# Six weight chunks held outside the ring, router logits taken from the residual rows, and the last norm done tile by tile

## The chip, the cores and the metric

The kernel runs on one core of one Trainium2 chip. The metric is device time in microseconds (us) of the whole kernel, lower is better. TensorE (PE) multiplies, VectorE (DVE) and ScalarE (ACT) do the elementwise work, SyncE (SP) issues most transfers, and 16 DMA engines move data between the device memory and the on-chip arena.

## What is computed

The program is two blocks in a row on 256 tokens of width 1024, all in f32: a transformer block of two layers, then a block of two layers whose second half is a mixture of experts. The change touches only the mixture of experts and the norm at the very end:

```
def ec_moe(h, router, wg, wu, wd):
    aff = softmax(h @ router)                      # 256 tokens x 16 experts
    gates, idx = top_k(swapaxes(aff, 1, 2), 32)    # each expert picks 32 tokens
    xs = h[idx]
    hid = silu(xs @ wg) * (xs @ wu)                # per expert, 1024 x 1024 each
    ys = hid @ wd * gates
    return zeros.at[idx].add(ys)
...
hx = rmsnorm_2(x, norm_g[i, 1]) * (1.0 + sc2x) + sh2x
x = x + g2x * ec_moe(hx, ...)
...
return rmsnorm_2(x, final_g)
```

Layer 0 runs this for two streams (x and ctx, four tiles of 128 tokens), the last layer for x alone (two tiles).

## The kernel before, in words

Weights come as one stream of chunks of 1 MB (128 partitions x 2048 f32) in the order of their use. `stream_weights` lets SP load them into a ring of six slots (`RING = 6`): SP waits on `chunks_used` until the chunk six places earlier has been read by PE, then issues the next transfer. PE waits for a chunk in `wait_chunk`. No other rule decides when a weight is loaded.

`experts(layer, ...)` is one stage of 4 + 192 chunks, each engine with its own program in written order, tied by the counting semaphores in `self.moe`:

- PE: `project(t)` multiplies by the output matrix of the mixer (4 chunks) for tile t; `turn_row(t)` transposes the normed tile `xn`; `logits(t)` multiplies the features `hT` by the router (8 products, which the trace shows as 16 PE instructions). Then come the turn of the softmax, `gate_rows`, and the first `gather` of tokens. Then 16 experts follow with 12 chunks each: chunks 0 to 3 (gate), 4 to 7 (up), 8 to 11 (down). `sum_expert(e - 1, ...)`, which scatters the expert before into the output banks, stands ahead of chunk 8.
- DVE adds the projected tile to the residual row (L1931, L1932), makes rstd and the normed tile, and does the softmax and the choice of tokens. ACT squares the row (L1877), takes the root, and writes the features out of PSUM with the scale and shift of the modulation, in 8 instructions of 128 columns for a tile (L1882). It issues the stage's small loads at its start (L1713, L1714).
- At the end `final_norm` starts with a `meet` of the engines (a wait on every semaphore so far), loads the gain `final_g` (L1469), squares both tiles, takes the mean, root and reciprocal of both, scales both (L368), and multiplies both by the gain (L1478). `store` has another `meet` on SP and then two transfers (L3189).

The clock of PE has two levels, 2.4 GHz (shown as a granted clock of 1.00) and 1.2 GHz (0.50).

## Time and profile before

| what | value |
|---|---|
| median of 3 runs | 3271.4 us (3271.13 to 3273.81) |
| the profiled execution's own time | 3272.74 us |
| its span, first to last instruction | 3270.7 us |
| PE busy, share of the span | 2856.5 us, 87% |
| DVE and ACT busy | 1155.4 us (35%), 999.8 us (31%) |
| mean granted clock of PE | 0.939 |
| moved by DMA | 708.64 MB, mean 217 GB/s |

The averages hide stages with different limits: the first two layers are full of PE work, and the two stages of experts stream 192 MB of weights each. The stage of layer 0 spans about 1448 to 2034 us, the last stage about 2712 us to the end. What an edit in one of them is worth has to be read there.

### The profile page before, as it was taken

What the parts mean: (1) busy time and instruction counts of PE and PEld (TensorE: products, weight loads), DVE (VectorE), ACT (ScalarE), POOL (GpSimd) and SP (SyncE); (2) the same over time, 40 slices, a digit from 0 to 9 for tenths busy, and PEclk for the clock granted to TensorE, in tenths of its full rate; (3) what the DMA queues carried; (4) which work ended last, traced back from release to release, by engine and by line L of the source; (5) the groups of instructions that cost most, each with busy time, mean ns of one, the idle gap of its engine ahead of it and who ended that gap; (6) DMA issues with size and microseconds to landing.
All of it is one profiled execution on the core that took longest, in us unless ns stands there. A gap on an engine that the chain in (4) does not pass through costs nothing.

```text
span 3270.7 us, 63075 instructions
## 1 busy us (share of the span) xinstructions
PE 2856.5 (87%) x27786; PEld 1880.1 (57%) x27786; DVE 1155.4 (35%) x1567; ACT 999.8 (31%) x1549; POOL 172.7 (5%) x229
## 2 busy tenths in 40 slices
PE   8999899999998899998998888998888887677765
PEld 6777677778676777755333223346777764332322
DVE  4445555455355565422000002334444433000001
ACT  4435544444345455323000001114444422000000
POOL 0001000000002000000000000002222210000000
PEclk9999999999999999998999999999999998777776
DMA  6463234565642354402999999611000014999997
GB/s 252 167 262 129 104 145 171 198 244 182 263 154 98 121 212 161 176 27 97 422 421 421 421 421 375 257 60 60 15 10 16 4 35 164 421 421 420 421 421 295
DMA packets 100989, 708.64 MB, mean 217 GB/s; under 512 B 11604, under 2 KB 12372, under 8 KB 17280
## 3 DMA queue, kind: packets, MB, share of 16 engines
q1 hardware_dynamic: 94320, 682.34, 52.8%
q10 hardware_dynamic: 5760, 19.91, 1.6%
q8 instruction: 219, 3.59, 0.4%
q0 software_dynamic: 656, 2.52, 0.2%
q14 instruction: 34, 0.28, 0.0%
HBM read 703.65 MB, written 1.07 MB: 215 GB/s over the span
## 4 chain that ended last, share of the span: by engine, by line
PE 63%; DMA 21%; DVE 6%; ACT 5%; issue 3%; POOL 1%; SPq 0%; DVEq 0%; ACTq 0%; POOLq 0%
DMA weight_ring<-in_stream 21%; PE banks L641 8%; PE banks L643 7%; PE banks L642 7%; PE banks L1859 7%; PE banks L2135 3%; PE banks L1740 3%; PE banks L957 3%; PE banks L959 2%; PE banks L958 2%; PE banks L2181 2%; PE banks L2554 1%; PE banks L2541 1%; PE banks L1086 1%; PE banks L2545 1%
## 5 line engine op out<-in xcount | busy, mean ns | idle before, releaser
L1859 PE MATMUL banks<-weight_ring,scratch 128*32 128x256 f32 (+1 forms) x4608 | 638.0, 535 | 185.8 <-DMA weight_ring<-in_stream 181.9
L1859 PEld LDWEIGHTS banks<-weight_ring,scratch 128*32 128x32 f32 (+1 forms) x4608 | 201.4, 134 | 603.1 <-DMA weight_ring<-in_stream 295.6
L638 DVE TENSOR_TENSOR split_high<-weight_ring,split_high 128x1024 fp32r<-128x1024 f32 x198 | 243.5, 1231 | 282.0 <-ACT split_high L633 280.6
L633 ACT CAST split_high<-weight_ring 128x1024 fp32r<-128x1024 f32 x198 | 207.9, 1052 | 312.6 <-PE banks L643 262.9
L1974 DVE TENSOR_TENSOR scratch<-scratch,banks 128x512 f32<-128x512 f32 (+1 forms) x32 | 17.7, 555 | 604.1 <-PE banks L1859 604.1
L1280 DVE TENSOR_TENSOR split_high<-weight_ring,split_high 128x1024 fp32r<-128x1024 f32 x128 | 160.0, 1256 | 199.1 <-ACT split_high L1175 198.7
L2883 ACT COPY scratch<-banks 128x512 f32<-128x512 f32 (+2 forms) x208 | 153.3, 767 | 230.0 <-PE banks L2545 132.2
L641 PE MATMUL banks<-split_high,features_low 128*128 128x512 f32 x528 | 210.8, 399 | 3.5 <-DVE features_low L560 3.5
L643 PE MATMUL banks<-split_high,features_high 128*128 128x512 f32 x528 | 207.3, 393 | 0.0
L642 PE MATMUL banks<-split_high,features_high 128*128 128x512 f32 x528 | 206.9, 392 | 0.0
L957 PE MATMUL banks<-split_high,features_low 128*128 128x512 f32 x416 | 170.6, 410 | 19.5 <-DVE split_high L1280 16.3
L1175 ACT CAST split_high<-weight_ring 128x1024 fp32r<-128x1024 f32 x128 | 133.2, 1047 | 135.6 <-PE banks L959 134.1
L1906 ACT ACTIVATE scratch<-banks 128x512 f32<-128x512 f32 (+1 forms) x32 | 15.7, 490 | 517.1 <-PE banks L1859 517.1
L958 PE MATMUL banks<-split_high,features_high 128*128 128x512 f32 x416 | 165.4, 398 | 0.0
L959 PE MATMUL banks<-split_high,features_high 128*128 128x512 f32 x416 | 165.3, 397 | 0.0
L1908 ACT COPY scratch<-banks 128x512 f32<-128x512 f32 (+1 forms) x32 | 15.3, 479 | 353.7 <-PE banks L1835 353.7
L638 DVE TENSOR_TENSOR scratch<-weight_ring,scratch 128x1024 fp32r<-128x1024 f32 x66 | 80.8, 1225 | 107.7 <-ACT scratch L633 107.4
L641 PEld LDWEIGHTS banks<-split_high,features_low 128*128 128x128 f32 x528 | 99.9, 189 | 26.4 <-issue 4.0
L643 PEld LDWEIGHTS banks<-split_high,features_high 128*128 128x128 f32 x528 | 99.9, 189 | 21.3
L642 PEld LDWEIGHTS banks<-split_high,features_high 128*128 128x128 f32 x528 | 100.0, 189 | 20.9
L641 PE MATMUL banks<-split_high,scratch 128*128 128x512 f32 x264 | 106.7, 404 | 2.8 <-DVE scratch L764 2.8
L957 PEld LDWEIGHTS banks<-split_high,features_low 128*128 128x128 f32 x416 | 80.0, 192 | 44.2 <-DVE split_high L1280 21.7
(381 smaller groups left out, 4687.5 us busy)
## 6 DMA issues: line engine op xcount, KB each, us to landing
weight_ring<-in_stream SPq DMA_DIRECT2D x648, 1024.0 KB, 11.3
scratch<-in_pair_rows ACTq DMA_DIRECT2D x8, 448.0 KB, 3.7
scratch<-in_lora ACTq DMA_DIRECT2D x2, 1536.0 KB, 17.1
front<-in_gain_rows ACTq DMA_DIRECT2D x5, 512.0 KB, 3.7
bias<-bias_rows POOLq DMA_DIRECT2D x1, 2304.0 KB, 13.7
scratch<-in_routing ACTq DMA_DIRECT2D x2, 1040.5 KB, 5.4
resid<-in_x SPq DMA_DIRECT2D x2, 512.0 KB, 3.9
resid<-in_ctx ACTq DMA_DIRECT2D x2, 512.0 KB, 5.6
```

Source lines behind the costliest of these rows:

```text
L633: act.copy(split[i % 4][0], source(i)).then_inc(*self.rounded.up())
L638: dve.tensor_tensor(lo, source(i), hi.bitcast(F32), ALU.subtract).then_inc(*self.rest.up())
L641: pe.matmul(out, lhs_lo, hi, start=start, stop=False)
L642: pe.matmul(out, lhs_hi, lo, start=False, stop=False)
L643: return pe.matmul(out, lhs_hi, hi, start=False, stop=stop)
L957: pe.matmul(out, lhs_lo, hi, start=start, stop=False)
L958: pe.matmul(out, lhs_hi, lo, start=False, stop=False)
L959: return pe.matmul(out, lhs_hi, hi, start=False, stop=stop)
L1175: act.copy(split[i % 3][0], source(i)).then_inc(*self.rounded.up())
L1280: dve.tensor_tensor(lo, source(i), hi.bitcast(F32), ALU.subtract).then_inc(*self.rest.up())
L1859: last = pe.matmul(self.psum[q * M:(q + 1) * M, (GATE, UP, DOWN)[part], 0:W], left, w[:, j * D + q * W:j * D + (q + 1) * W], start=(k == 0 ...
L2883: act.copy(dst, src).then_inc(*done.up())
```

## The change

Four things change, all but the last two in `experts`.

1. Chunks 6 to 11 of expert 0 of the last stage are taken out of the stream. They are an input of their own, `kept`, and ACT loads them at the begin of the stage into six free pieces of the arena. PE reads them there; the stream has six chunks less, so chunk 0 of expert 1 follows chunk 5 of expert 0 in the ring.
2. The logits are made from the residual row before its norm: `turn_row` transposes `row(t)` and waits for `rowed` where it waited for `normed`; ACT copies the transposed tile in one instruction; DVE scales the router once (`scaled`) and afterwards multiplies the logits by rstd and adds an offset, the product of shift and router, for which PE has 8 more products for each stream (`offsets`).
3. `sum_expert(e - 1, ...)` moves from ahead of chunk 8 to ahead of chunk 4.
4. The last norm: its gain is loaded with the stage's small loads, the squares of a tile start as its row is ready, and gain and rstd are applied by one instruction for a tile. SP waits for each tile alone.

```diff
-        gate = [A[:, 30780 + D * s:30780 + D * (s + 1)] for s in range(S)]
+        gate = [A[:, 30780 + D * s:30780 + D * (s + 1)] for s in range(2)] if layer == 0 else [A[:, 28864:29888]]
+        kept = [A[:, o:o + CHUNK] for o in ((6144, 14336, 2048, 10240, 29888, 31936) if layer else ())]
...
+            else:
+                act.dma_start(gain, io["final_g"].to_broadcast([P, D])).then_inc(*self.params_loaded.dma())
+                for i, w in enumerate(kept):
+                    act.dma_start(w, io["kept"][i]).then_inc(*self.kept_loaded[i // 2].dma())
...
             def turn_row(t):
-                wait(pe, "normed", t + 1)
+                wait(pe, "rowed", t + 1)
...
+            def offsets(s):
+                if s == 0:
+                    wait(pe, "scaled", 1)
+                for k in range(KT):
+                    pe.matmul(self.psum[:, 0 if S == 2 else 4, (n_t + s) * NE:(n_t + s + 1) * NE], self.modcol[:, 3, s, k:k + 1].to_broadcast([P, P]),
+                              router[:, k, :], start=(k == 0), stop=(k == KT - 1))
...
+            for s in range(S):
+                offsets(s)
             turn_row(n_t - 1)
             logits(n_t - 2)
             logits(n_t - 1)
...
                     if c == 4 and e:
                         wait(pe, "weighted", e)
+                        wait(pe, "ys", e)
+                        for t in range(1 if S == 2 else TT):
+                            sum_expert(e - 1, t, SUM)
...
-                        if e:
-                            wait(pe, "ys", e)
-                            for t in range(1 if S == 2 else TT):
-                                sum_expert(e - 1, t, SUM)
                         wait(pe, "hid_saved", e + 1)
...
-                    n = e0 + 12 * e + c
-                    self.wait_chunk(pe, n)
-                    w = self.slot(n)
+                    at = 12 * e + c
+                    n = e0 + at - (0 if at < RING else len(kept))
+                    own = not RING <= at < RING + len(kept)
+                    if own:
+                        self.wait_chunk(pe, n)
+                        w = self.slot(n)
+                    else:
+                        pe.wait_ge(self.kept_loaded[(at - RING) // 2].sem, 32)
+                        w = kept[at - RING]
...
-                for k in range(KT):
-                    last = act.activation(hT[:, k, t * P:(t + 1) * P], self.psum[:, 2 * t + k // 4, (k % 4) * P:(k % 4 + 1) * P],
-                                          ACT.Identity, bias=self.modcol[:, 3, s, k:k + 1], scale=self.scol[:, 1, s, k:k + 1])
-                last.then_inc(*up("featured"))
+                act.copy(hT[:, :, t * P:(t + 1) * P].rearrange("p (a k) c -> p a k c", a=2),
+                         self.bank(2 * t, 2).rearrange("p a (k c) -> p a k c", k=4)).then_inc(*up("featured"))
...
+            dve.wait_ge(self.params_loaded.sem, loaded)
+            for s in range(S):
+                last = dve.tensor_tensor(scaled[:, s], router, bc(self.scol[:, 1, s, :], NE), ALU.mult)
+            last.then_inc(*up("scaled"))
             for t in range(n_t):
...
             wait(dve, "logits", 1)
-            then(dve.tensor_reduce(by_tile[0], logits, AX.X, ALU.max))
-            dve.tensor_tensor(aff, logits, bc(by_tile[0], NE), ALU.subtract).then_inc(*up("less_max"))
+            dve.tensor_copy(offset, self.psum[:, 0 if S == 2 else 4, n_t * NE:(n_t + S) * NE].rearrange("p (s e) -> p s e", s=S)).then_inc(*self.ve.up())
+            then(dve.tensor_tensor(aff, by_stream, bc(rstd.rearrange("p (s t) -> p t s", s=S), NE), ALU.mult))
+            then(dve.tensor_tensor(aff, aff, offset.unsqueeze(1).to_broadcast([P, TT, S, NE]), ALU.add))
+            then(dve.tensor_reduce(by_tile[0], aff, AX.X, ALU.max))
+            dve.tensor_tensor(aff, aff, bc(by_tile[0], NE), ALU.subtract).then_inc(*up("less_max"))
...
+                def scale(t):
+                    dve.wait_ge(self.row_rooted.sem, norm0[self.row_rooted] + t + 1)
+                    then(dve.reciprocal(rstd[:, t:t + 1], roots[:, t:t + 1]))
+                    dve.scalar_tensor_tensor(out=out[:, t, :], in0=row(t), scalar=rstd[:, t:t + 1], in1=gain, op0=ALU.mult, op1=ALU.mult)\
+                        .then_inc(*self.row_normed.up())
+
+                finish(0)
+                finish(1)
+                mean(0)
+                scale(0)
+                mean(1)
+                scale(1)
...
         @self.block.sync
         def _(sp):
-            self.meet(sp)
             for t in range(TT):
+                self.outputs(sp, t)
                 sp.dma_start(io["out"][t * P:(t + 1) * P], out[:, t, :]).then_inc(*self.stored.dma())
```

Three places show how the instructions move. The first is PE in layer 0, from the transposes of tile 2 on to the softmax's turn. L1750 (L1743 in the changed kernel) is `turn_row`, L1759 (L1752) `logits`, L1761 `offsets`. Before:

```order
L1750 MATMUL banks<-ident,scratch_0 128x128 x8
L1759 MATMUL banks<-scratch_0 128x16 x8
L1750 MATMUL banks<-ident,scratch_0 128x128 x8
L1759 MATMUL banks<-scratch_0 128x16 x16
L1801 MATMUL banks<-ident,small 32x128 x2
```

and in the changed kernel:

```order
L1743 MATMUL banks<-ident,resid 128x128 x8
L1752 MATMUL banks<-scratch_0 128x16 x8
L1761 MATMUL banks<-scratch_0,small 128x16 x16
L1743 MATMUL banks<-ident,resid 128x128 x8
L1752 MATMUL banks<-scratch_0 128x16 x16
L1803 MATMUL banks<-ident,small 32x128 x2
```

The 16 products of the offsets stand ahead of the transposes of the last tile, where PE had nothing queued. The last stage has the same order with half as many (8).

The second place is PE in expert 0 of the last stage, from chunk 5 to chunk 0 of expert 1, with its waits. L1859 (L1866) is the expert product; a wait on `slot_loaded` is one for the ring. Before:

```order
L1859 MATMUL banks<-weight_ring,scratch_0 32x256 [waits slot_loaded5]
L1859 MATMUL banks<-weight_ring,scratch_0 32x256 x7
L1859 MATMUL banks<-weight_ring,scratch_0 32x256 [waits slot_loaded0]
L1859 MATMUL banks<-weight_ring,scratch_0 32x256 x7
L1859 MATMUL banks<-weight_ring,scratch_0 32x256 [waits slot_loaded1]
L1859 MATMUL banks<-weight_ring,scratch_0 32x256 x7
L1772 MATMUL banks<-scratch_0 128x128 [waits moe_selected,moe_silu]
L1772 MATMUL banks<-scratch_0 128x128 x3
L1835 MATMUL banks<-ident,scratch_0 128x128 [waits moe_hid]
L1835 MATMUL banks<-ident,scratch_0 128x128
L1859 MATMUL banks<-weight_ring,scratch_0 32x256 [waits slot_loaded2,moe_hid_saved]
```

and in the changed kernel:

```order
L1866 MATMUL banks<-weight_ring,scratch_0 32x256 [waits slot_loaded5]
L1866 MATMUL banks<-weight_ring,scratch_0 32x256 x7
L1866 MATMUL banks<-scratch_0 32x256 [waits kept_loaded0]
L1866 MATMUL banks<-scratch_0 32x256 x7
L1866 MATMUL banks<-scratch_0 32x256 [waits kept_loaded0]
L1866 MATMUL banks<-scratch_0 32x256 x7
L1772 MATMUL banks<-scratch_0 128x128 [waits moe_selected,moe_silu]
L1772 MATMUL banks<-scratch_0 128x128 x3
L1840 MATMUL banks<-ident,scratch_0 128x128 [waits moe_hid]
L1840 MATMUL banks<-ident,scratch_0 128x128
L1866 MATMUL banks<-scratch_0 32x256 [waits kept_loaded1,moe_hid_saved]
```

PE's work is the same, but the six chunks 6 to 11 no longer wait for the ring; their waits are on `kept_loaded0` to `kept_loaded2`.

The third place is DVE from the last sums to its last instruction. Before (L1990 and L1991 add an output tile to the residual row, L368 scales by rstd, L1478 by the gain):

```order
L1990 TENSOR_TENSOR scratch_0<-banks,scratch_0 128x1024
L1991 TENSOR_TENSOR resid<-resid,scratch_0 128x1024
L1990 TENSOR_TENSOR scratch_0<-banks,scratch_0 128x1024
L1991 TENSOR_TENSOR resid<-resid,scratch_0 128x1024
L350 UNCONDITIONAL_BRANCH
L354 TENSOR_SCALAR small<-small 128x2
L362 UNCONDITIONAL_BRANCH
L365 RECIPROCAL small<-small 128x2
L368 TENSOR_SCALAR scratch_0<-resid,small 128x1024 x2
L1478 TENSOR_TENSOR scratch_0<-scratch_0 128x1024 x2
```

and in the changed kernel:

```order
L2014 TENSOR_TENSOR scratch_0<-banks,scratch_0 128x1024
L2016 TENSOR_TENSOR resid<-resid,scratch_0 128x1024
L2020 TENSOR_SCALAR small<-small 128x1
L2024 RECIPROCAL small<-small 128x1
L2025 SCALAR_TENSOR_TENSOR scratch_0<-resid,small,scratch_0 128x1024
L2020 TENSOR_SCALAR small<-small 128x1
L2024 RECIPROCAL small<-small 128x1
L2025 SCALAR_TENSOR_TENSOR scratch_0<-resid,small,scratch_0 128x1024
```

Four long instructions after the last sum become two, and each tile has its own mean and reciprocal.

## Rows read from the trace of the kernel before

In rows of the timeline the first two numbers are the start and the length in us, then engine, line, operation, output<-input and count; in brackets is the idle time before and what ended it. In rows of windows they are the stretch, its length, the busy time (and count) of PE, PEld, DVE, ACT and POOL, the granted clock of PE, the busy share of the DMA engines, and GB/s.

**Rows 1.** The page: GB/s moved, in 40 equal slices of the span

```profile
GB/s 252 167 262 129 104 145 171 198 244 182 263 154 98 121 212 161 176 27 97 422 421 421 421 421 375 257 60 60 15 10 16 4 35 164 421 421 420 421 421 295
```

**Rows 2.** Windows: one in each stage of experts, and two near the end

```profile
1900.00:2000.00 100.00, 84.06 (x374) 24.72 (x370) 6.86 (x12) 4.14 (x7) 0.00 (x0) 1.00 1.01 421
...
2900.00:3000.00 100.00, 70.92 (x740) 30.40 (x730) 5.68 (x13) 5.22 (x15) 0.00 (x0) 0.75 1.01 421
...
3246.00:3248.00 2.00, 1.89 (x33) 0.89 (x32) 0.95 (x3) 0.00 (x0) 0.00 (x0) 1.00 0.03 8
```

**Rows 3.** Timeline of expert 0 and the first ring rounds of the last stage

```profile
2775.05 5.39 PE L1859 MATMUL banks<-weight_ring,scratch 128*32 128x256 f32 x96 [0.90 <-ACT scratch L1898]
2776.33 53.57 SPq L328 DMA_DIRECT2D weight_ring<-in_stream  x25
...
2785.07 1.93 PE L1859 MATMUL banks<-weight_ring,scratch 128*32 128x256 f32 x16 [2.81 <-DMA weight_ring<-in_stream]
...
2799.98 1.07 PE L1859 MATMUL banks<-weight_ring,scratch 128*32 128x256 f32 x16 [1.31 <-DMA weight_ring<-in_stream]
...
2814.91 1.07 PE L1859 MATMUL banks<-weight_ring,scratch 128*32 128x256 f32 x16 [0.58 <-DMA weight_ring<-in_stream]
```

**Rows 4.** Timeline of layer 0, from the logits of tile 1 to the softmax

```profile
1507.55 1.86 PE L1759 MATMUL banks<-scratch 128*128 128x16 f32 x16
...
1508.13 1.23 DVE L1932 TENSOR_TENSOR resid<-resid,scratch 128x1024 f32<-128x1024 f32 x1
...
1513.14 1.97 PE L1750 MATMUL banks<-ident,scratch 128*128 128x128 f32 x8 [3.74 <-DVE scratch L1937]
...
1514.91 6.84 PE L1759 MATMUL banks<-scratch 128*128 128x16 f32 x32
...
1521.79 0.23 DVE L1942 TENSOR_REDUCE small<-banks 128x4 f32<-128x64 f32 x1 [8.70 <-PE banks L1759]
```

**Rows 5.** Timeline of the last stage, from the transposes of tile 0 to the softmax

```profile
2743.57 1.04 PE L1750 MATMUL banks<-ident,scratch 128*128 128x128 f32 x8
...
2745.03 1.22 DVE L1932 TENSOR_TENSOR resid<-resid,scratch 128x1024 f32<-128x1024 f32 x1
2747.39 1.09 ACT L1877 ACTIVATE scratch<-resid 128x1024 f32<-128x1024 f32 x1
...
2750.04 1.97 PE L1750 MATMUL banks<-ident,scratch 128*128 128x128 f32 x8 [5.44 <-DVE scratch L1937]
...
2758.69 0.19 DVE L1942 TENSOR_REDUCE small<-banks 128x2 f32<-128x32 f32 x1 [8.70 <-PE banks L1759]
```

**Rows 6.** Windows of 5 us over the same places of both stages

```profile
1510.00:1515.00 5.00, 1.85 (x10) 1.86 (x10) 1.07 (x3) 1.89 (x5) 0.00 (x0) 0.53 0.23 98
1515.00:1520.00 5.00, 5.00 (x26) 5.00 (x25) 0.00 (x0) 4.18 (x9) 0.00 (x0) 0.50 0.00 0
...
2745.00:2750.00 5.00, 0.00 (x0) 0.00 (x0) 2.30 (x4) 3.78 (x11) 0.00 (x0) 0.93 0.50 197
```

**Rows 7.** Timeline of the last expert and what follows it

```profile
3239.87 2.09 PE L1785 MATMUL banks<-scratch 32*128 32x256 f32 x16
...
3253.31 1.23 DVE L1991 TENSOR_TENSOR resid<-resid,scratch 128x1024 f32<-128x1024 f32 x1
...
3263.09 2.36 DVE L1478 TENSOR_TENSOR scratch<-scratch 128x1024 f32<-128x1024 f32 x2
3266.39 0.83 SPq L3189 DMA_DIRECT2D out_x<-scratch  x2
```

**Rows 8.** One line's instructions: durations in ns, least, median, most

```profile
L554 DVE SCALAR_TENSOR_TENSOR front<-resid,small,front x12: 1283/1285/1286, 11.0 to 1183.3; 128x1024 f32<-128x1024 f32 x12
```

**Rows 9.** Timeline at the begin of the last stage: loads by ACT

```profile
2730.30 0.46 ACTq L1714 DMA_DIRECT2D scratch<-in_routing  x1
```

**Rows 10.** DMA issues: count, KB each, median us to landing

```profile
scratch<-in_lora ACTq DMA_DIRECT2D x2, 1536.0 KB, 17.1
scratch<-in_routing ACTq DMA_DIRECT2D x2, 1040.5 KB, 5.4
```

More of the change, by code:

```diff
@@ L243, in __init__ @@
         self.early |= {"ctx_turned": self.moe["row_turned"], "gate_saved": self.moe["gate_saved"], "row_finished": self.moe["rowed"]}
+        self.kept_loaded = [signal(f"kept_loaded{i}") for i in range(3)]
         self.rowed = signal("row_ready")
@@ L1459 @@
     MOD = 34064
-    def final_norm(self, name, dst):
-        nc, ve = self.nc, self.ve
-        xn, gain = self.tiles(0, TT, D), self.arena[:, 2048:3072]
-        @self.block.scalar
-        def _(act):
-            self.meet(act)
-            act.dma_start(gain, self.io[name].to_broadcast([P, D])).then_inc(*self.params_loaded.dma())
-        loaded = self.params_loaded.count
-        self.norm_rows([0, 1], xn)
-        @self.block.vector
-        def _(dve):
-            dve.wait_ge(ve.sem, ve.count)
-            dve.wait_ge(self.params_loaded.sem, loaded)
-            for t in range(TT):
-                nc.vector.tensor_tensor(dst(t), xn[:, t, :], gain, ALU.mult).then_inc(*ve.up())
     def ada_chunk(self, pe, chunk, k, cT, bank):
@@ L1699, in experts @@
         tile_of = [(s, t) for s in range(S) for t in range(TT)]
+        gain, out = A[:, 17408:18432], self.tiles(0, TT, D)
         base = {n: s.count for n, s in self.moe.items()}
+        norm0 = {s: s.count for s in (self.rowed, self.row_squared, self.row_meant, self.row_rooted, self.row_normed)}
         before = self.so_far()
@@ L1870, in _ @@
                 last.then_inc(*up("summed"))
-        self.chunk = e0 + MOE_CHUNKS
+        self.chunk = e0 + MOE_CHUNKS - len(kept)
         @self.block.scalar
@@ L1911, in _ @@
             act.activation(self.small[:, 16:17], self.ident[:, 0:1], ACT.Sqrt).then_inc(*self.se.up())
+            if S == 1:
+                for t in range(TT):
+                    act.wait_ge(self.rowed.sem, norm0[self.rowed] + t + 1)
+                    act.activation(out[:, t, :], row(t), ACT.Square, accum_out=sums[:, t:t + 1]).then_inc(*self.row_squared.up())
+                for t in range(TT):
+                    act.wait_ge(self.row_meant.sem, norm0[self.row_meant] + t + 1)
+                    act.activation(roots[:, t:t + 1], sums[:, t:t + 1], ACT.Sqrt).then_inc(*self.row_rooted.up())
         @self.block.vector
@@ L1972, in _ @@
                 wait(dve, "silu", e + 1)
-                dve.wait_ge(self.chunks_used.sem, e0 + 12 * e + 8)
+                if kept and e == 0:
+                    wait(dve, "kept_up", 1)
+                else:
+                    dve.wait_ge(self.chunks_used.sem, e0 + 12 * e + 8 - len(kept))
                 dve.tensor_tensor(hid[:, e % 2, 0:W], silu[:, e % 2, 0:W], self.psum[:, UP, 0:W], ALU.mult).then_inc(*up("hid"))
@@ L1978, in _, with finish, mean @@
                                          op0=ALU.is_equal, op1=ALU.mult).then_inc(*up("weighted"))
-                dve.wait_ge(self.chunks_used.sem, e0 + 12 * e + 12)
+                if kept and e == 0:
+                    wait(dve, "kept_down", 1)
+                else:
+                    dve.wait_ge(self.chunks_used.sem, e0 + 12 * e + 12 - len(kept))
                 dve.tensor_copy(ys[:, e, :], self.psum[:, DOWN, 0:W]).then_inc(*up("ys"))
-            for i in range(S):
+            if S == 1:
+                def finish(t):
+                    wait(dve, "summed", TT)
+                    then(dve.tensor_tensor(xn[:, t, :].rearrange("p (q d) -> p q d", q=Q), self.psum[:, SUM:SUM + Q, t * W:(t + 1) * W],
+                                           gate[0].rearrange("p (q d) -> p q d", q=Q), ALU.mult))
+                    dve.tensor_tensor(row(t), row(t), xn[:, t, :], ALU.add).then_inc(*self.rowed.up())
+                def mean(t):
+                    dve.wait_ge(self.row_squared.sem, norm0[self.row_squared] + t + 1)
+                    dve.tensor_scalar(sums[:, t:t + 1], sums[:, t:t + 1], 1.0 / D, EPS, ALU.mult, ALU.add).then_inc(*self.row_meant.up())
+                def scale(t):
[9 more added lines that the diff above has]
+                scale(1)
```

45 lines of the change are left out of this document (26 added, 19 removed).

## The prediction, made before the changed kernel ran

> **What bounds the kernel now.** I read the page's slices first: both stages of experts run at 421 to 422 GB/s, the rest far below [rows 1]. The windows say what PE does meanwhile: in layer 0 it is busy 84 of 100 us at full clock, in the last stage 71 of 100 us at a mean clock of 0.75, and the DMA engines are at 1.01 in both [rows 2]. So the stream bounds these stages, with PE slack, and what counts is when the stream starts to run and how many chunks it has. Then the timeline at both ends. In the last stage PE starts expert 0 at 2775.05 with six chunks in the ring, SP issues the next at 2776.33, and from then on PE waits for DMA: the chunk at 2799.98 and the one six later at 2814.91 are 14.93 us apart, 2.49 us a chunk [rows 3]. Ahead of that stands the routing, a chain of small work in which the stream is idle: no byte moves in 1515 to 1520 us [rows 6]. Behind it stands a tail in which nothing is loaded.
>
> **1. Six chunks outside the ring.** PE reads chunks 0 to 5 and 6 to 11 of expert 0 without the ring; the ring restarts at the same point, but has 180 chunks instead of 186. If it never runs dry, the last chunk lands 6 x 2.49 = 14.9 us earlier. One condition: the seventh new chunk needs the slot of chunk 0 of expert 1, so PE must be through expert 0 before the six slots are full. The chunk of 2799.98 is the eighth after the restart, so the sixth lands at 2795.0, 19.9 us after PE's start, and SP must issue the next some 2 us before. PE needs 5.4 us for chunks 0 to 5, then six more at 1.07 us (full clock, as at 2799.98) or 1.93 us (half, as at 2785.07) [rows 3], the gather, two turns and spread, some 3 to 5 us, and 1 to 2 us for chunk 0 of expert 1: 16 us at full clock, 23 us at half. PE is at full clock there before and has no wait now, so I take 16 and no stall. Bounds: 14.9 us to 14.9 - 5.3 us.
>
> The six transfers are issued by ACT from about 2731 us on, behind the stage's small loads. With four ring chunks they are 10 MB, 25 us at 421 GB/s, so all is there by 2757 us, and the first kept chunk is read after 2776. The idle stream hides them. The DMA page of the Trainium skill ("DMA: Bandwidth & Descriptors", Bandwidth) has loads from HBM held to about 358 GB/s for a core; by that a chunk were 2.93 us and the six worth 17.6 us, and the time 2.7 us lower. This trace's 421 GB/s contradicts it, and the trace decides.
>
> **2. Logits from the residual row, last stage: 4.4 us gained.** Now tile 1's row is ready at 2745.03 + 1.22 = 2746.25, and PE stands until 2750.04 for square, root and normed tile; transposes and 32 logit instructions then run at half clock, and DVE starts the softmax at 2758.69 [rows 5]. After: PE ends tile 0's transposes at 2744.6 [rows 5], then the offsets: 16 instructions. At full clock one takes 1.86 / 16 = 0.116 us, at half 6.84 / 32 = 0.214 us [rows 4]. So offsets to 2746.5, transposes of tile 1 to 2747.55 (1.04 us as tile 0's), logits of tile 0 from there. ACT squares the row in 1.09 us [rows 5] and copies the features by 2749.1, in time. The clock is the open point. In layer 0 PE ran the last projection, transposes and 1.86 us of logits [rows 4], and the clock fell in the window 1510 to 1515 (0.53); the last stage's fell near the end of 2745 to 2750 (0.93) [rows 6]. And PE stood at 0.50 while busy 5.00 of 5.00 us with logits [rows 6]: this work didn't raise it. So I let the clock fall amid the logits, at about 2748.5: 8 instructions at 0.116, 24 at 0.214, end 2753.6, against 2758.69. That is 5.1 us. DVE has three more small instructions (0.19 to 0.23 us each [rows 4, 5] and the step between them): 0.7 us back. Sum 4.4 us; bounds 1.3 (all at half clock) and 6.7 us (all at full).
>
> **3. The same in layer 0: 2.4 us lost.** Here the offsets are 32 instructions, and tile 3's row is ready at 1508.13 + 1.23 = 1509.36, just as PE ends the logits of tile 1 at 1509.41 [rows 4]. The offsets go first. Before, the transposes started at 1513.14 [rows 4]. With the clock falling near 1511, 14 offsets at full and 18 at half clock take 5.5 us, to 1514.9: 1.8 us later than before, and the rest runs at half clock as it did. With 0.7 us for DVE that is 2.4 us lost. Bounds: 3.8 us lost (all at half) and 3.2 us gained (all at full: offsets 3.7, transposes 1.04, logits 3.7 us, end 1517.9 against 1521.79, less 0.7).
>
> The new wait: DVE waits at the head of the stage for all small loads before it makes the scaled router, and tile 0's row is queued behind it, then PE's transposes. In layer 0 the loads have 13 us of projection ahead. In the last stage routing is issued at 2730.30 [rows 9] and lands in 5.4 us [rows 10]; the gain behind it is 0.5 MB more, 1.2 us, and ring chunks share the engines from about 2733, so 2738.5. Router and tile 0's row take 2.7 us more, to 2741.2; PE wants it at 2743.57 [rows 5]. Hidden, with 2.4 us to spare. ACT spends some 3 us more on issuing, and its square for tile 0 has until 2744. Costed at nothing.
>
> **4. sum_expert earlier.** It leaves the end of each expert: 2.09 us in the last one [rows 7]. Inside the stages the stream hides both places. In the last expert of either stage chunk 8 starts earlier, until the hidden tile's copy, and in the last stage until chunk 11's landing: almost nothing moves after 3246 (8 GB/s [rows 2]), so about there. I take 0.8 us for both stages; bounds 0 and 3.
>
> **5. The tail: 7.4 us.** The last sum's row ends at 3253.31 + 1.23 = 3254.54, the span at 3270.7: 16.2 us, with the gain's load, the squares, two passes over both tiles, the meet, and two stores [rows 7]. After: square of tile 1 to 3255.75 (tile 0's ran beside the sums), root and reciprocal 0.4, one fused pass of 1.28 [rows 8] to 3257.5, mean, root and reciprocal of tile 1 0.6, pass of 1.28 to 3259.4. From the issue of the second store to the end before: 3270.7 - 3266.81 = 3.9 us [rows 7], so 3263.3. Gain 7.4 us; bounds 6 and 8.
>
> **Sum.** 14.9 + 4.4 - 2.4 + 0.8 + 7.4 = 25.1 us. The profiled execution took 3272.7 us, so 3247.6; it is 1.3 us above the median of 3271.4, so 3246.3 us.
>
> **The rivals.**
>
> A. The clock stays up through the routing, as PE now has no gap. Layer 0 then gains 3.2 instead of losing 2.4, the last stage 6.7 instead of 4.4: 7.9 us more, 3238.4 us. For it: no idle time is left between projection and logits. Against: [rows 6], as above. The Trainium skill's page "TensorE: Matmul & The Clock Gate" (Part 1) has the clock given back by sustained activity and taken by idleness, which speaks for this case; the busy 1515 to 1520 us at 0.50 speak against it. Chance 0.13.
>
> B. The ring runs dry behind expert 0, because PE needs 23 us at half clock: 5.3 us lost, 3251.6 us. Against: full clock there in the trace. Chance 0.12.
>
> C. The small loads of the last stage land late and DVE's new wait exceeds its cover. Loads queued by ACT together can take 17.1 us (lora, [rows 10]); then row 0 comes at 2750.6, 7 us after 2743.6: 3253.3 us. "DMA: Bandwidth & Descriptors" of the Trainium skill (Queues, rings and completion order) lets every DMA engine alternate between queues, which makes the ring a competitor here; no row shows the shares. Chance 0.10.
>
> D. The stage isn't as free as it looks: PE becomes the bound once the stream is ahead, and the six chunks bring nothing. Then 3261.2 us. Against: PE's 29 idle us of 100 [rows 2]. Chance 0.05.
>
> E. Slower: the kept transfers crawl. At lora's 1.57 MB in 17.1 us, 92 GB/s, 6.3 MB take 68 us, the last pair lands at 2799 and PE, which would start expert 0 at 2770.6, wants it 12 us later: 16 to 17 us late, of which the ring forgives 3, so 3246.3 + 14 = 3260. It decides below 79 GB/s (80 us, 28 late, all 25 us gone); at 70 GB/s it is 38 late, 3246.3 + 35 = 3281 us. Against: lora was one of four loads issued together beside the ring. Chance 0.03.
>
> **Numbers.** The forecast has 0.55; the 0.02 left I give to no change that can be told. Its own range is 3242 to 3251. For 8 in 10 I add most of A and C: 3239 to 3253. A measurement of this kernel can tell about 0.2%, 6.5 us: only E lies on the slow side, and D is 10 us off and still faster. Faster 0.95, within 0.2% 0.02, slower 0.03.
>
> **What would show it.** Right: in the last stage SP's issues run without a pause after expert 0, chunk cadence 2.49 us, and from PE's start of expert 0 to the last chunk 14.9 us less; no wait on the kept chunks; offsets between transposes in both stages, with 0.116 and then 0.214 us each; the softmax of layer 0 about 2 us later than before, counted from the last projection, and that of the last stage 5 us earlier; about 8.8 us from the last sum to the end. Wrong: a wait of DVE for loads that reaches past 2743.6, a hole in the stream some 20 us after expert 0 starts, full clock through the logits, or a wait for a kept chunk.

## The result and the profile after

The changed kernel took 3242.5 us in the median of 4 runs (3237.7 to 3250.2), the kernel before 3271.6 us (3271.1 to 3273.8) beside it: a ratio of 0.9907, 95% interval 0.9894 to 0.9921. The forecast was 3246.3, its own range 3242 to 3251. The profiled execution took 3243.30 us, 29.44 us less than the 3272.74 of the one before.

To see where they come from I cut each profile at eight events of the timelines: start and end of layer 0's projection (the first transposes behind it), the Exp of its softmax, PE's first product of its expert 0, and in the last stage the transposes of tile 0, the Exp, expert 0, the last DVE copy of an expert, the last residual add, and the span's end. In us:

| stretch | before | after | gained |
|---|---|---|---|
| up to layer 0's projection (untouched) | 1448.10 | 1447.21 | 0.89 |
| that projection (untouched) | 58.57 | 58.58 | 0.0 |
| layer 0: transposes to Exp | 15.64 | 16.49 | -0.85 |
| layer 0: Exp to expert 0 | 18.63 | 20.28 | -1.65 |
| layer 0's experts to the last stage's transposes | 1202.63 | 1201.22 | 1.4 |
| last stage: transposes to Exp | 15.57 | 8.89 | 6.7 |
| last stage: Exp to expert 0 | 15.91 | 14.54 | 1.4 |
| expert 0 to the last copy: the stream | 472.91 | 459.44 | 13.5 |
| last copy to last add | 5.35 | 5.86 | -0.5 |
| last add to the end | 17.4 | 8.9 | 8.5 |

**The six chunks.** Below is the timeline of PE and of SP's queue from expert 0 of the last stage on, after; it answers to [rows 3].

```profile
2767.21 5.39 PE L1866 MATMUL banks<-weight_ring,scratch 128*32 128x256 f32 x96 [0.90 <-ACT scratch L1908]
2772.42 1.91 PE L1866 MATMUL banks<-scratch 128*32 128x256 f32 x32
...
2780.77 3.64 PE L1866 MATMUL banks<-weight_ring,scratch 128*32 128x256 f32 x64
...
2787.35 1.07 PE L1866 MATMUL banks<-weight_ring,scratch 128*32 128x256 f32 x16 [0.87 <-DMA weight_ring<-in_stream]
2789.81 1.07 PE L1866 MATMUL banks<-weight_ring,scratch 128*32 128x256 f32 x16 [1.40 <-DMA weight_ring<-in_stream]
...
2768.49 45.85 SPq L330 DMA_DIRECT2D weight_ring<-in_stream  x22
```

PE reads chunks 0 to 5, then two kept ones at 2772.42 with no wait; the other four, at 2776.10 and 2779.02, wait for no load either. It is at chunk 0 of expert 1 at 2780.77, 13.6 us after its start, so that slot is free about 14.5 us after it, where 16 was forecast and some 18 were allowed. The waits for DMA begin at 2787.35 and stand 2.5 us apart, as before, with no hole. The kept transfers are issued from 2731.49 on; their landings, and that of the gain, stand in the answer on DMA issues between 2720 and 2800 (KB each, median us to landing):

```profile
scratch<-in_kept ACTq DMA_DIRECT2D x6, 1024.0 KB, 22.3
...
scratch<-in_final_g ACTq DMA_DIRECT2D x1, 512.0 KB, 7.2
```

Before, the ring was full by about 2748 and nothing moved until PE began expert 0. The window of before, with the DMA share and GB/s in its last two columns:

```profile
2750.00:2775.00 25.00, 19.00 (x80) 16.37 (x80) 7.37 (x26) 8.64 (x19) 0.00 (x0) 0.60 0.00 1
```

The windows after, two over layer 0's routing and four over the last stage's, show that idle stream in use (up to about 2761.5; the forecast had 2757 and left out the small loads), and in front of the last two columns PE's granted clock, on which the next parts rest:

```profile
1510.00:1515.00 5.00, 5.00 (x32) 5.00 (x31) 0.92 (x2) 0.57 (x2) 0.00 (x0) 0.63 0.04 16
1515.00:1520.00 5.00, 5.00 (x25) 5.00 (x25) 0.00 (x0) 1.80 (x2) 0.00 (x0) 0.50 0.00 0
...
2745.00:2750.00 5.00, 4.99 (x46) 4.89 (x45) 2.51 (x5) 4.13 (x6) 0.00 (x0) 1.00 1.02 429
2750.00:2755.00 5.00, 3.06 (x14) 2.35 (x14) 2.11 (x10) 0.51 (x2) 0.00 (x0) 0.54 1.01 419
2755.00:2760.00 5.00, 2.46 (x4) 0.52 (x2) 4.62 (x15) 1.01 (x1) 0.00 (x0) 0.78 1.02 423
2760.00:2765.00 5.00, 4.18 (x24) 4.08 (x25) 1.09 (x5) 1.24 (x4) 0.00 (x0) 0.66 0.33 136
```

**The last stage's routing.** The timeline of DVE, then of PE; it answers to [rows 5].

```profile
2738.31 0.29 DVE L1945 TENSOR_TENSOR small<-scratch,small 128x128 f32<-128x128 f32 x1 [17.24 <-DMA scratch<-in_final_g]
...
2751.70 0.17 DVE L1963 COPY small<-banks 128x16 f32<-128x16 f32 x1 [2.63 <-PE banks L1752]
...
2743.78 1.04 PE L1743 MATMUL banks<-ident,resid 128*128 128x128 f32 x8
2744.66 1.86 PE L1761 MATMUL banks<-scratch,small 128*128 128x16 f32 x16
2746.53 1.09 PE L1743 MATMUL banks<-ident,resid 128*128 128x128 f32 x8
2747.45 4.21 PE L1752 MATMUL banks<-small,scratch 128*128 128x16 f32 x32
```

DVE's new wait ends at 2738.31 (forecast 2738.5), and PE finds tile 0's row at 2743.78. PE then has no gap up to the end of the logits, and the 32 logit instructions take 4.21 us, near the 3.7 of full clock and far from the 6.84 of half: the clock stayed at 1.00 to 2750, and fell when PE was almost through. Full clock through the logits was one of the forecast's own signs of being wrong; here it held for most of them, and in two later profiles (after_again and mix_logits, 3.64 us) for all.

**Layer 0's routing**, PE and then DVE, against [rows 4]:

```profile
1508.37 4.32 PE L1761 MATMUL banks<-scratch,small 128*128 128x16 f32 x32
1512.53 1.95 PE L1743 MATMUL banks<-ident,resid 128*128 128x128 f32 x8
1514.27 6.85 PE L1752 MATMUL banks<-scratch 128*128 128x16 f32 x32
...
1521.15 0.19 DVE L1963 COPY small<-banks 128x32 f32<-128x32 f32 x1 [10.09 <-PE banks L1752]
```

The offsets run first at full and then at half clock, and tile 3's row waits behind them.

**The tail**, PE, DVE and SP's queue, against [rows 7]:

```profile
3224.70 1.90 PE L1866 MATMUL banks<-weight_ring,scratch 128*32 128x256 f32 x16 [1.32 <-DMA weight_ring<-in_stream]
...
3232.51 1.22 DVE L2016 TENSOR_TENSOR resid<-resid,scratch 128x1024 f32<-128x1024 f32 x1
...
3235.24 1.28 DVE L2025 SCALAR_TENSOR_TENSOR scratch<-resid,small,scratch 128x1024 f32<-128x1024 f32 x1
...
3237.06 1.28 DVE L2025 SCALAR_TENSOR_TENSOR scratch<-resid,small,scratch 128x1024 f32<-128x1024 f32 x1
...
3236.56 2.17 SPq L3238 DMA_DIRECT2D out_x<-scratch  x2
```

From the last add's end (3232.51 + 1.22 = 3233.73) to the span's end (3241.4) are 7.7 us, where 8.8 were forecast.

### The profile page after: what moved, and what is told of

Same layout as the page of the kernel before. It is cut to its first block, busy times and chain, and to the rows that moved or that the text cites. A ratio compares the mean times of both kernels' runs of the same rounds, so it can differ in the third digit from the quotient of the medians.

```text
span 3241.4 us, 63061 instructions
## 1 busy us (share of the span) xinstructions
PE 2829.0 (87%) x27834; PEld 1871.6 (58%) x27834; DVE 1156.9 (36%) x1576; ACT 988.9 (31%) x1508; POOL 172.9 (5%) x229
## 4 chain that ended last, share of the span: by engine, by line
PE 64%; DMA 21%; DVE 6%; ACT 5%; issue 3%; POOL 1%; SPq 0%; DVEq 0%; ACTq 0%; POOLq 0%
DMA weight_ring<-in_stream 21%; PE banks L643 8%; PE banks L645 7%; PE banks L644 7%; PE banks L1866 7%; PE banks L1733 3%; PE banks L2184 3%; PE banks L959 3%; PE banks L961 2%; PE banks L960 2%; PE banks L2230 2%; PE banks L2603 1%; PE banks L2590 1%; PE banks L1772 1%; PE banks L1088 1%
## 5 line engine op out<-in xcount | busy, mean ns | idle before, releaser
L1866 PE MATMUL banks<-weight_ring,scratch 128*32 128x256 f32 (+1 forms) x4512 | 602.9, 507 | 196.8 <-DMA weight_ring<-in_stream 174.7
L1866 PEld LDWEIGHTS banks<-weight_ring,scratch 128*32 128x32 f32 (+1 forms) x4512 | 189.4, 129 | 576.3 <-DMA weight_ring<-in_stream 318.8
L1918 ACT COPY scratch<-banks 128x512 f32<-128x512 f32 (+1 forms) x32 | 15.3, 479 | 348.6 <-PE banks L1840 348.6
## 6 DMA issues: line engine op xcount, KB each, us to landing
scratch<-in_kept ACTq DMA_DIRECT2D x6, 1024.0 KB, 22.3
```

The costliest lines, as they stand in the source:

```text
L1866: last = pe.matmul(self.psum[q * M:(q + 1) * M, (GATE, UP, DOWN)[part], 0:W], left, w[:, j * D + q * W:j * D + (q + 1) * W], start=(k == 0 ...
```

## The experiments

The theory: the stream gains by the number of kept chunks, 2.49 us each; the routing gains in the last stage because PE no longer waits for the norm and the clock stays up, and loses in layer 0 by the work added; the tail is the shorter chain. The rivals: the gain in the stream comes from `sum_expert` or elsewhere; the differences of a us or two are the clock's chance. Times are medians of the runs. The first four kernels shared 14 runs of the kernel before (3272.2 us), the next four 7 (3268.8), the last two 9 (3273.8). The stretches of the table above tell more than the medians; here they are in us, from one profile of each kernel (kept_first's last column holds the 21.45 us hole told of below):

| run | median | layer 0 to Exp | to expert 0 | last stage to Exp | to expert 0 | stream | last add to end | layer 0's experts to last stage, untouched |
|---|---|---|---|---|---|---|---|---|
| after_again | 3247.4 | 18.25 | 20.15 | 8.32 | 15.27 | 458.04 | 8.9 | 1200.2 |
| no_kept | 3256.7 | 18.21 | 20.19 | 9.45 | 15.66 | 475.99 | 8.9 | 1194.9 |
| old_logits | 3244.7 | 15.64 | 20.55 | 15.57 | 15.91 | 459.32 | 8.9 | 1192.4 |
| old_sum | 3244.8 | 18.27 | 18.63 | 8.62 | 14.80 | 458.15 | 8.9 | 1198.9 |
| kept8 | 3233.9 | 18.27 | 18.64 | 9.10 | 15.97 | 454.01 | 8.9 | 1195.9 |
| mix_logits | 3243.0 | 15.64 | 18.63 | 8.33 | 15.25 | 459.68 | 8.9 | 1204.5 |
| kept_first | 3279.2 | 18.24 | 20.15 | 14.63 | 16.04 | 459.64 | 8.9 | 1226.3 |
| old_tail | 3251.6 | 18.23 | 20.16 | 9.58 | 15.53 | 457.99 | 17.4 | 1198.5 |
| best | 3238.8 | 15.64 | 18.63 | 9.09 | 15.97 | 453.59 | 8.9 | 1202.0 |
| best_warm | 3237.0 | 15.64 | 19.61 | 9.44 | 13.18 | 455.04 | 8.9 | 1201.4 |

**after_again**, the changed kernel unchanged.

> The changed kernel itself, to see what varies: its four runs lay between 3237.7 and 3250.2 us, those of the kernel before within 2.7 us. Theory 1 (the half clock of PE falls at a moment that differs between runs, and the changed routing carries more PE work there): a second profile differs from the first in the routing of both stages by up to 6 us in layer 0 and 3 us in the last stage, and its stream in the last stage is as long (459 us from PE's start of expert 0 to the last copy of the last expert). Theory 2 (PE is sometimes at half clock in expert 0, and the ring runs dry): this stretch is up to 5 us longer in a slower run, with a hole in the stream some 20 us after expert 0 starts. Theory 3: the difference lies in stages that the change doesn't touch.

3247.4 us (3245.0 to 3255.1, 6 runs), ratio 0.9928 (0.9913 to 0.9944). Its profile took 3.9 us more than the first one of the same kernel: 5.0 us of it lie before layer 0's projection (1452.25 against 1447.21), where nothing was changed. So theory 3 holds for most of the difference. Of theory 1, layer 0's routing is 1.8 us longer up to the Exp and the last stage's 0.6 us shorter; of theory 2 there is nothing, the stream is 1.4 us shorter. Single times of one kernel can't size a term of a few us; stretches can.

**no_kept**, the chunks back in the ring.

```diff
-        kept = [A[:, o:o + CHUNK] for o in ((6144, 14336, 2048, 10240, 29888, 31936) if layer else ())]
+        kept = []
```

> The changed kernel with all 192 chunks of the last stage in the ring, the rest as changed. Theory (the stream bounds the stage, six chunks are 14.9 us): 14.9 us slower than the changed kernel, 3257.4 us, and from PE's start of expert 0 to the last copy 473 us instead of 459.4. Rival (the six chunks only fill a start that PE would have caught up): 5 us slower or less. Rival (the kept transfers cost something themselves, by contention with the small loads): less than 14.9 us, with DVE's first row of the last stage earlier than the 2738.3 us of the changed kernel (8.4 us after the projection of the last tile starts).

3256.7 us (3255.1 to 3264.4), ratio 0.9956 (0.9944 to 0.9969). PE waits where it found kept chunks before:

```profile
2768.19 5.39 PE L1866 MATMUL banks<-weight_ring,scratch 128*32 128x256 f32 x96 [0.90 <-ACT scratch L1908]
2775.65 1.31 PE L1866 MATMUL banks<-weight_ring,scratch 128*32 128x256 f32 x16 [2.07 <-DMA weight_ring<-in_stream]
2778.37 1.94 PE L1866 MATMUL banks<-weight_ring,scratch 128*32 128x256 f32 x16 [1.41 <-DMA weight_ring<-in_stream]
```

The stream takes 475.99 us. Two profiles without kept chunks give 472.9 and 476.0, seven with six of them 458.0 to 459.7: 13.2 to 18.0 us between them, 15.6 between the means, and 14.9 was forecast. The medians are only 9.2 us apart (no_kept against after_again); in the profiles 5.3 us of the difference is taken back by the untouched stretch. The second rival is real but small and hidden: DVE's wait for the loads ends 7.3 us after the start of the last tile's projection, against 7.6 to 8.4 with kept chunks behind the same loads, and in each case PE wants the row later.

**old_logits**, both routings as before (normed tiles, no offsets), all else changed.

```diff
-                wait(pe, "rowed", t + 1)
+                wait(pe, "normed", t + 1)
...
-            for s in range(S):
-                offsets(s)
```

> The changed kernel with the logits as before the change: transposes of the normed tile, features by 8 scaled instructions, no offsets, softmax from the plain logits. Theory (the new logits cost about 2.5 us in layer 0 and save 5 to 8 us in the last stage, net 2 to 5.5 us saved): 3244.5 to 3248 us. Layer 0 from the end of the last projection to the first expert product takes 34.3 us as in the kernel before instead of 36.8, the last stage from the transposes of tile 0 to the first expert product 31.5 instead of 23.4 us. Rival (the layer 0 loss is only the clock's chance): layer 0 takes about as long with the old logits. The spread of the runs is that of the kernel before (under 3 us) if theory 1 of the spread holds.

3244.7 us (3241.4 to 3247.4), ratio 0.9919 (0.9901 to 0.9937). The stretches to Exp are again those of before to 0.01 us, 15.64 and 15.57. So the new logits lose 2.6 us in layer 0 (0.85 in the first profile) and gain 6.0 to 7.2 in the last stage up to the Exp. The medians show nothing of it: 3244.7 lies between the two of the changed kernel, 3242.5 and 3247.4, and the profile's untouched stretch was 8 to 9 us shorter.

**old_sum**, `sum_expert` back ahead of chunk 8.

> The changed kernel with the sum of the expert before back ahead of chunk 8. Theory (the stream hides it inside the stages, and at their ends the last chunk's landing decides): 0 to 1 us slower, the last expert's chunk 8 starts 1.5 us later and chunk 11 under 0.5 us later. Rival (it matters in each expert, since PE catches up with the ring faster): 3 us slower or more.

3244.8 us (3239.8 to 3253.9), ratio 0.9926 (0.9906 to 0.9946); the stream 458.15 us, inside the other profiles' range. As expected PE begins chunk 8 of the last expert 1.5 us sooner in the changed kernel (counted from the transposes of the hidden tile), but then waits 1.32 us for chunk 11 (line of 3224.70 above), where old_sum has no wait. The move brings nothing that these runs can tell.

**mix_logits**, the old routing in layer 0 alone.

```diff
-            for s in range(S):
+            for s in range(S if layer else 0):
```

> The changed kernel with the new logits in the last stage only, the old ones in layer 0. Theory (in layer 0 PE never stands, so the offsets' 32 instructions go on its path): from the end of layer 0's last projection to its softmax 15.6 us as in the kernel before, against 16.5 and 18.3 us in the two profiles of the changed kernel; the last stage keeps its 8.3 to 8.9 us. About 1 to 2.7 us less in all, which the spread of whole runs (some 10 us) may hide. Rival (only the clock's chance): layer 0 takes 16.5 us or more here too.

3243.0 us (3241.0 to 3249.9), ratio 0.9916 (0.9885 to 0.9947): 15.64 us in layer 0 and 8.33 in the last stage, the better half of each. The spread of the medians hides the gain, as was expected.

**kept8**, chunks 0 and 1 of expert 1 kept too, issued by ACT once it has copied the features.

```diff
-KEPT = 6
+KEPT = 8
...
+            if kept:
+                for i in (6, 7):
+                    act.dma_start(kept[i], io["kept"][i]).then_inc(*self.kept_loaded[2].dma())
```

> The changed kernel with eight chunks outside the ring instead of six: chunks 0 and 1 of expert 1 as well, loaded by ACT after it has written the features of the last tile. Theory (the stream bounds the stage and its start is the free resource): two chunks less, 5.0 us off the stretch from PE's start of expert 0 to the last copy (454 instead of 459 us), provided that PE has used chunk 2 of expert 1, the first it takes from the ring again, within some 18 us of its start (in the changed kernel chunk 0 of expert 1 was used after 14.5 us, so 16.5 us are expected). Rival (the six slots run full before that and the ring has a hole): 1 to 4 us of the 5 come back as a hole some 20 us after the start.

3233.9 us (3233.1 to 3239.1), ratio 0.9896 (0.9864 to 0.9927), the stream 454.0 us: two more chunks, 4.9 us less than the mean with six (4.0 to 5.7 against the single profiles).

```profile
2762.68 5.39 PE L1867 MATMUL banks<-weight_ring,scratch 128*32 128x256 f32 x96 [0.90 <-ACT scratch L1912]
...
2774.48 3.66 PE L1867 MATMUL banks<-scratch 128*32 128x256 f32 x64
2777.96 1.91 PE L1867 MATMUL banks<-weight_ring,scratch 128*32 128x256 f32 x32
...
2788.40 1.07 PE L1867 MATMUL banks<-weight_ring,scratch 128*32 128x256 f32 x16 [1.02 <-DMA weight_ring<-in_stream]
```

PE is back in the ring 15.3 us after its start, still ahead of the sixth slot's landing. The idle stream is nearly used up, though: around PE's start of expert 0 the DMA engines stand for some 3 us, where they stood about 6 us in the changed kernel and over 25 in the kernel before. The window of that stop:

```profile
2761.00:2764.00 3.00, 2.10 (x32) 1.40 (x35) 0.00 (x0) 2.61 (x5) 0.00 (x0) 1.00 0.04 14
```

**kept_first**, the six transfers issued ahead of the stage's small loads instead of behind them, in the same queue: rival C made certain.

```diff
+            for i, w in enumerate(kept):
+                act.dma_start(w, io["kept"][i]).then_inc(*self.kept_loaded[i // 2].dma())
...
-                for i, w in enumerate(kept):
-                    act.dma_start(w, io["kept"][i]).then_inc(*self.kept_loaded[i // 2].dma())
```

> The changed kernel with the six kept chunks issued by ACT ahead of the stage's small loads instead of behind them. It takes the cover of DVE's new wait away. Theory (loads of one queue land in their order, and DVE's wait then decides): 6.3 MB at 421 GB/s shared with the ring's chunks from about 2733, so the small loads land some 18 to 22 us later than 2738.3, at 2756 to 2760; tile 0's row, and with it PE's transposes, start 15 us or more after the end of the last projection, and the routing of the last stage is about 14 to 17 us longer. Rival (the transfers of one queue share the engines evenly): the small loads come only 5 to 10 us later and the routing is under 8 us longer.

One run, 3279.2 us, over 24 us more than any run of the changed kernel, and inside the range of the seven runs of the kernel before beside it (3260.7 to 3282.6). The timeline of ACT's queue, DVE and PE, and a window:

```profile
2737.55 3.01 ACTq L1703 DMA_DIRECT2D scratch<-in_kept  x6
...
2741.63 0.50 ACTq L1711 DMA_DIRECT2D scratch<-in_final_g  x1
...
2770.05 0.29 DVE L1945 TENSOR_TENSOR small<-scratch,small 128x128 f32<-128x128 f32 x1 [41.57 <-DMA scratch<-in_final_g]
...
2772.79 1.97 PE L1743 MATMUL banks<-ident,resid 128*128 128x128 f32 x8 [21.45 <-DVE resid L1953]
...
2755.00:2760.00 5.00, 0.00 (x0) 0.00 (x0) 0.00 (x0) 0.00 (x0) 0.00 (x0) 0.50 1.02 424
```

DVE's wait now ends 28.4 us after the gain's issue, which in the changed kernel landed in 7.2, PE stands 21.45 us, and at half clock behind it the routing takes 14.63 us to the Exp instead of 8.9. Counted from the start of the last tile's projection the wait ends 24.4 us later than in the changed kernel, where 18 to 22 were forecast, and wait and routing together are 27 us longer, where 14 to 17 were: PE's hole came out longer, and the forecast left out the half clock behind it. The rival, under 8 us, is out. By the stretches of this one profile the order of six issues in one queue is worth about as much as the whole change.

**old_tail**, the last norm as before.

> The changed kernel with the old last norm: gain loaded at the end, meets, both tiles together, two passes, and the meet of SP ahead of the stores. Theory (the tail's edit is worth 7.4 to 8.5 us by itself): from the start of the last sum to the end 17.4 us as in the kernel before, against 8.9 us. Rival (part of the gain came from the stage ahead): under 7 us more.

One run, 3251.6 us. The timeline from the last add:

```profile
3232.07 1.23 DVE L2035 TENSOR_TENSOR resid<-resid,scratch 128x1024 f32<-128x1024 f32 x1
3233.71 0.33 ACTq L1471 DMA_DIRECT2D scratch<-in_final_g  x1
3237.02 1.06 ACT L349 ACTIVATE scratch<-resid 128x1024 f32<-128x1024 f32 x1 [16.14 <-DMA scratch<-in_final_g]
...
3241.82 2.36 DVE L1480 TENSOR_TENSOR scratch<-scratch 128x1024 f32<-128x1024 f32 x2
3245.12 0.83 SPq L3253 DMA_DIRECT2D out_x<-scratch  x2
```

17.4 us to the end of the span (3249.5), as before, against 8.9 in all kernels with the new tail: 8.5 us.

**best** (kept8 with mix_logits) and **best_warm**, which adds PE products where PE would wait for DVE; nobody reads their results:

```diff
+            def keep_warm(n):
+                for _ in range(n):
+                    pe.matmul(self.psum[:, 7, :], self.ident[:, :], self.resid[:, 0:NB], start=True, stop=True)
```

> Eight kept chunks in the last stage, and layer 0's routing again as in the kernel before (normed tiles, logits in one product each); the rest as changed. If the parts add up: layer 0 from projection's end to the softmax's Exp 15.6 us instead of 16.5 to 18.3, the last stage as in the run with eight kept chunks (about 8.9 us to Exp, 454 us from expert 0 to the last chunk), the tail 8.9 us. That is 0.9 to 2.6 us below the 3233.9 of eight kept chunks: 3231 to 3233 us. Rival: layer 0's routing trades its gain for its clock afterwards (an Exp to first expert product of 20.2 us instead of 18.6), and the kernel stays at 3233 to 3235.

> As the run before it, with dummy products whose results nobody reads (128x512 on a free bank, one ahead of the gate rows, two or one ahead of the gathers, in both layers) that PE makes where it would stand and wait for DVE. Theory that the clock in the routing falls because PE idles: the clock there stays nearer 1.00, gate rows and gathers take 1.98 and 5.2 us rather than 3.6 and 6.5, and Exp to the first expert product is 18.6 us in layer 0 and 13 to 14.5 in the last stage in every profile; 0 to 3 us gained on the run before. Rival: the dummies only delay PE by 0.2 to 0.9 us a place and the clock moves as it did: 0 to 2 us lost.

3238.8 us (3234.3 to 3244.6, ratio 0.9896, 0.9877 to 0.9914) and 3237.0 us (3236.4 to 3238.4, ratio 0.9887, 0.9871 to 0.9903). best has each stretch that its parts promised, 15.64, 9.09 and 453.6 us, and missed its forecast in absolute time for the same reason as the others: its untouched stretch is 6 us longer than kept8's. Against the kernel before, best is level with kept8 (0.9896 both), and its interval overlaps that of the changed kernel's first ratio (0.9894 to 0.9921): that layer 0's old routing saves time is shown by the stretch alone. The windows of best and then of best_warm, over the gathers of the last stage:

```profile
2755.00:2760.00 5.00, 2.24 (x5) 0.53 (x3) 4.42 (x13) 1.01 (x1) 0.00 (x0) 0.84 1.02 424
2760.00:2765.00 5.00, 4.19 (x21) 4.11 (x20) 1.09 (x5) 1.10 (x3) 0.00 (x0) 0.50 1.02 424
```

```profile
2755.00:2760.00 5.00, 4.95 (x10) 2.09 (x10) 4.01 (x14) 1.01 (x1) 0.00 (x0) 0.75 1.02 423
2760.00:2765.00 5.00, 2.77 (x24) 2.63 (x24) 2.42 (x8) 1.15 (x3) 0.00 (x0) 1.00 1.01 423
```

With the dummies PE is busy through 2755 to 2760, the clock is 1.00 behind it, and the 32 gather products take 3.84 us instead of 6.63:

```profile
2760.89 6.63 PE L1775 MATMUL banks<-scratch 128*128 128x128 f32 x32 [0.81 <-DVE scratch L2003]
```

```profile
2762.57 3.84 PE L1775 MATMUL banks<-scratch 128*128 128x128 f32 x32 [0.81 <-DVE scratch L2009]
```

The eleven profiles without dummies have 5.20 to 6.70 us there. That makes 2.8 us from the Exp to expert 0, but little is left of it. Layer 0 gives back 1.0 (19.61 against 18.63: the clock came back without help, and a dummy product stands in PE's way), the stretch to the last stage's Exp 0.4 and the stream 1.4 (455.04 against 453.59), so that the two spans are level, 3236.2 and 3236.6 us. Why the stream is longer no run shows; the DMA engines' stop at the start of expert 0, some 3 us in best, is down to about 1.5, with a share of 0.12:

```profile
2767.50:2769.00 1.50, 1.50 (x32) 0.91 (x28) 0.00 (x0) 1.05 (x1) 0.00 (x0) 1.00 0.12 44
```

These are one profile of each; the runs, with medians 1.8 us apart, overlap.

## Why the prediction was right, point by point

- **Six chunks, 14.9 us forecast.** 13.5 in the first pair of profiles, 15.6 between the means, 2.5 a chunk again for the two of kept8. Shown by taking the chunks away and by adding two. Their transfers are hidden by the idle stream, and only as long as they stand behind the small loads (kept_first). The 17.6 us that the Trainium skill's 358 GB/s would give lie inside the single differences, but the steady stretch runs at 421 GB/s. The same section of the Trainium skill ("DMA: Bandwidth & Descriptors", Bandwidth) has about 358 GB/s as the share of each of two cores that stream together, and 425 GB/s for one core alone. This program runs on one core, and its 421 agrees with the second figure.
- **Last stage's routing, 4.4 us forecast, 6.7 measured** to the Exp, the upper bound of the term. The step that was off is "I let the clock fall amid the logits, at about 2748.5": it fell behind 2750, when some 27 of the 32 instructions were through. What I read from layer 0, where it fell sooner, did not carry over, and the moment varies: over the eight other profiles with the new logits and a full clock ahead of them the stretch is 8.3 to 9.6 us. Another 1.4 us behind it, most of it in the gathers (5.20 us for 6.47), is clock too, and varies as much from profile to profile (14.5 to 16.0 us from the Exp to expert 0 without dummies). best_warm suggests, in one profile, that it depends on what PE does while it waits.
- **Layer 0's routing, 2.4 us lost forecast.** 2.6 us in all six other profiles that have it; 0.85 in the first, whose offsets took 4.32 us and not 5.5: this first profile had luck with the clock. Behind it, 1.65 us more went to the second pair of gate rows at half clock (3.63 us for 1.98), at which the forecast put nothing. Five of the seven profiles with the new routing in layer 0 have some 20.2 us there and two 18.6 (old_sum, kept8); of the four with the old one and no dummies three have 18.6 and one 20.55 (old_logits). So it isn't bound to the change, but whether the later softmax makes it likelier stays open.
- **sum_expert, 0.8 us forecast:** nothing that can be told; what the earlier chunk 8 wins is waited away at chunk 11.
- **Tail, 7.4 us forecast, 8.5 measured** (old_tail undoes it alone; the other kernels with the new tail agree to 0.1). The chain was right; "3.9 us" from the second store's issue to the end was the size that was off, since the pass ends at 3238.34 and the span 3.1 us later. The 0.5 us lost before it (the last sum's 16 products take 1.66 us for 1.15) are clock.
- **The sum, 25.1 us forecast, 29.4 between the two profiles,** of which 2.3 lie in untouched stretches. The terms missed both ways. The stream was forecast 1.4 us too high and `sum_expert` with the stretch behind the last copy 1.3 too high; the two routings up to the Exp came out 2.3 and 1.6 us better and the tail 1.1 better than forecast. The clock behind each Exp, for which there was no term, cost 1.65 us in layer 0 and gave 1.4 in the last stage. That the whole came within 4.3 us is partly luck, as is the median's place in its range: the same kernel had 3247.4 in its second series. Rival A held in the last stage, for most of the logits, and not in layer 0. B: PE had 14.5 us of work, not 23. C is real but wasn't met: the wait ended at 2738.31, tile 0's row was ready at 2741.0 and PE took it at 2743.78. D fell with the 2.5 us a chunk, E with landings of 22.3 us in the median.
- **Open:** the untouched stretches move by 6 us ahead of layer 0's projection (1446.2 to 1452.3) and by 12 us between layer 0's experts and the last stage (1192 to 1204), from kernel to kernel and run to run. The profiles show where: layer 0's experts themselves take 471.5 to 472.7 us in all of them, and what moves is the stretch behind, up to the last stage's transposes. It goes with PE's granted clock: 720.7 us at a mean of 0.981 (old_logits), 723 to 726 us at 0.974 to 0.976 (no_kept, kept8, old_tail, old_sum), 729 to 732 us at 0.965 to 0.972 (the others but kept_first, whose hole lies in it). Ahead of layer 0 it is 1446.2 to 1449.5 us at 0.978 to 0.981 and 1451.2 to 1452.3 at 0.975 to 0.976. What makes the clock differ there was not tried, nor whether this is all of the 4.9 us between the two medians of the changed kernel.

## What to carry to other kernels

Where weights stream through a ring and the stream idles during a serial stage, each chunk of otherwise free memory loaded there takes one chunk's transfer time off the end, as long as the consumer comes back to the ring before its slots are full and the stream has idle time left there (over 25 us before, about 6 with six chunks, 3 with eight). Put such bulk loads behind every small load of the same queue on which something waits: the same six transfers ahead of them cost 27 us in one profile, where they had brought some 15. Weigh moving work ahead of a norm by what PE has to do at that moment: with two tiles it filled a wait, with four it stood in the way.

## What the runs showed of the hardware

TensorE's clock fell while PE was busy: with 5.00 of 5.00 us of logits, offsets and transposes it was at 0.63 in 1510 to 1515 and 0.50 in 1515 to 1520. In best_warm, with the dummy products in 2755 to 2760, it was at 1.00 in 2760 to 2765, where best had 0.50. The page "TensorE: Matmul & The Clock Gate" of the Trainium skill (Part 1) ties the clock to sustained activity; best_warm agrees; in the two windows of layer 0 the clock is low all the same, with PE's record busy throughout.

The stream ends at half rate, before and after. The windows ahead of its end, before the change and then after:

```profile
3235.00:3240.00 5.00, 3.82 (x34) 1.21 (x26) 0.42 (x1) 0.02 (x1) 0.00 (x0) 0.50 1.01 421
3240.00:3245.00 5.00, 5.00 (x49) 2.50 (x49) 0.00 (x0) 1.84 (x3) 0.00 (x0) 0.57 0.54 226
```

```profile
3212.00:3217.00 5.00, 2.99 (x34) 1.02 (x26) 0.42 (x1) 0.00 (x0) 0.00 (x0) 0.76 1.02 424
3217.00:3222.00 5.00, 4.54 (x36) 2.07 (x36) 0.00 (x0) 1.86 (x3) 0.00 (x0) 0.56 0.55 228
```

The 16 engines have a mean share of 0.55 and move 228 instead of 424 GB/s. Over the last 1.3 MB or so that is, by an estimate from these rates, about 3 us more than at the full rate, and after the change PE waits 1.32 us of it for the last chunk (3224.70). Why was not tried.
